# Alternating the units of two experts one by one inside a step of a two-expert SwiGLU loop

## The chip, the cores and the metric

The kernel runs on one core of a Trainium2 chip. The metric is the device time of one execution in microseconds, the median of several runs. The profile comes from one further execution.

## The reference, cut to what matters

The program is a two-layer decoder trunk on 256 tokens of width 1024. Layer 0 has windowed attention and a dense SwiGLU; layer 1 has dilated attention and a SwiGLU of eight experts, of which each token uses two. The change lies in the experts alone:

```python
def swiglu(h, w_gate, w_up, w_down):
    a = jnp.einsum('bsd,df->bsf', h, w_gate)
    b = jnp.einsum('bsd,df->bsf', h, w_up)
    return jnp.einsum('bsf,fd->bsd', jax.nn.silu(a) * b, w_down)

for e in range(N_EXPERTS):
    y = y + combine[..., e:e + 1].astype(h.dtype) * swiglu(h, w_gate[e], w_up[e], w_down[e])
```

All is float32. `D_FF` is 3584, so one expert has three matrices of 1024 x 3584.

## The kernel before, in words

**Three products for one.** A float32 product is made of fp32r products: each weight is split into a high part (`whi`, written by ScalarE in `cut`, line 548) and the rest (`wlo`, written by VectorE in its own `cut`, line 918, as raw minus `whi`). The activations have `xhi` and `xlo`, or `thi` and `tlo`. TensorE then forms hi x hi, hi x lo and lo x hi (`three`, lines 1470 to 1472).

**Units.** The weights are moved in units of 128 x 2048 values, 1 MB each. SyncE loads a unit into one of six `raw` buffers (line 414) as soon as VectorE has split the unit six places before (`lo_ready`). ScalarE splits it into one of four `whi` buffers, and waits for that until TensorE has finished the unit four places before (`units_done`); VectorE writes one of three `wlo` buffers, and waits for ScalarE's part (`hi_ready`) and for TensorE to have finished the unit three places before. TensorE waits for `lo_ready`.

**Pairs.** The experts are taken two by two, in four pairs here: a large one with up to 128 tokens and a small one with up to 64. A unit of the large expert is 12 matmuls of 512 columns (`unit_in`, `large_out`). For the small expert the high and the low part of the tokens stand side by side in one stationary tile, so its unit is 8 matmuls (`small_in` lines 1869 to 1873, `small_out` lines 1880 and 1881). A unit of either costs the same to load and to split.

**Steps.** 3584 columns are worked off in seven pieces of 512. Of each, an expert has two units of `moe_up`, two of `moe_gate` and two of `moe_down`. The loop `for s in 1..6` of every engine takes 12 units, called c to c+11 here with `c = MOE0 - 4 + 12 s`: up of piece s of the large expert (c, c+1), up of the small one (c+2, c+3), gate of the large (c+4, c+5), of the small (c+6, c+7), down of piece s-1 of the large (c+8, c+9) and of the small (c+10, c+11). A pair is eight units ahead of the loop, six steps, and four units behind it: 84 units.

**What hangs between the units.** The large expert: ScalarE `large_silu` (line 799) once its gate is done, VectorE `large_mul` (line 1365), TensorE `large_t` (four transposes, line 1919), ScalarE `large_thi` (line 804), VectorE `large_tlo` (line 1370). The small expert: `fold` at the end of a step (lines 1907 and 1911), VectorE `small_up` (line 1376), ScalarE `small_silu` (line 815), VectorE `small_mul` (line 1382), ScalarE `small_thi` (line 820), VectorE `small_tlo` (line 1388).

**What sets the order.** Every engine's order is written out by hand and is strict. In ScalarE's loop body the last three pieces are the split of c+12, `large_thi`, the split of c+13; in VectorE's the first are the split of c, `large_tlo`, the split of c+1, `small_up`, the split of c+2, `small_mul`, the splits of c+3 and c+4, `small_tlo`. So ScalarE's split of c+13 stands behind a wait for the transposes of `large_t`, and VectorE's split of the same unit (its c+1 of the next step) stands behind `large_tlo`.

```python
for i in range(11, 13):
    cut(c + i, rs)
large_thi(pair, s)
cut(c + 13, rs)
```

Of the kernel before, what the change touches and what calls it, by code (L numbers as in the profile page):

```python
# [35 lines left out]
STEPS = DFF // FCH  # L36
# [45 lines left out]
FIRST, FFN0, MOE0 = plan_units()  # L82
# [83 lines left out]
def trunk(nc, x, mem, rel_bias_table, mem_norm, norm_mix, norm_ffn, final_norm, swa_w_in, swa_sinks,  # L166
# [8 lines left out]
    moe_in = [w.rearrange("u p f -> p u f") for w in (moe_up, moe_gate)]  # L175
# [7 lines left out]
    with ctx:  # L183
# [221 lines left out]
        @block.sync  # L405
        def _(sp):
            for t in range(TILES):
                sp.dma_start(memx[:, t, :], mem[0, t * P:(t + 1) * P, :]).then_inc(mem_in[t], 16)

            def load(c, rounds, src):  # L410

                wait(sp, lo_ready, c + RAW * rounds - RAW + 1)
                dst = raw[:, c % RAW, 0:span(c)].rearrange("p (k f) -> p k f", k=src.shape[-2])
                sp.dma_start(dst, src).then_inc(raw_full[c % RAW], 16)

            def chunk_unit(k, i):

                name, width, rows_, off = CHUNKS[k]
                w = chunk_w[name]
                return bass.AP(w.tensor, w.offset + off * rows_ * P + i * P * 4 * width, [[4 * width, P], [1, 1], [1, 4 * width]])  # L420

            def load_chunks(lo, hi):
                for k in range(lo, hi):
                    for i in range(CHUNKS[k][2] // 4):
                        load(FIRST[k] + i, 0, chunk_unit(k, i))

            for half in range(2):
                piece = slice(half * 1024, half * 1024 + 1024)
                sp.dma_start(raw[:, 0:1, piece], chunk_unit(0, 0)[:, :, piece]).then_inc((first_in, raw_full[0])[half], 16)
            load(1, 0, chunk_unit(0, 1))  # L430
            load(2, 0, chunk_unit(1, 0))
            sp.dma_start(h[:, :, :], x[0].rearrange("(t p) d -> p t d", p=P)).then_inc(x_in, 16)
            sp.dma_start(gain[:, 1, :], bass.AP(gains[1].tensor, gains[1].offset, [[0, P], [1, D]]))\
                .then_inc(x_gain_in, 16)
            load(3, 0, chunk_unit(1, 1))
            load_chunks(C_SI, C_DI)

            for i in range(4):
                load(FFN0 + i, 0, ffn_in[i // 2][:, i % 2:i % 2 + 1, :])
            with sp.Fori(1, STEPS) as s:  # L440
                for i in range(4):
                    load(FFN0 - 2 + i, s, ffn_in[i // 2][:, bass.ds(2 * s + i % 2, 1), :])
                for i in range(2):
                    load(FFN0 + 2 + i, s, ffn_out[:, bass.ds(2 * s - 2 + i, 1), :])
            for i in range(2):
                u = 2 * STEPS - 2 + i
                load(FFN0 + FFN_UNITS - 2 + i, 0, ffn_out[:, u:u + 1, :])
            load_chunks(C_DI, len(CHUNKS))

            def load_in(c, rounds, first_unit):  # L450

                for i in range(4):
                    load(c + i, rounds, moe_in[i // 2][:, bass.ds(first_unit + i % 2, 1), :])

            def load_two(c, rounds, w, first_unit):

                for i in range(2):
                    load(c + i, rounds, w[:, bass.ds(first_unit + i, 1), :])

            def load_steps(pair, a, b):  # L460
                r = ROUNDS * pair
                load_in(MOE0 + 4, r, b)
                with sp.Fori(1, STEPS) as s:
                    for g in range(2):
                        load_two(MOE0 - 4 + 4 * g, r + 2 * s, moe_in[g], a + 2 * s)
                        load_two(MOE0 - 2 + 4 * g, r + 2 * s, moe_in[g], b + 2 * s)
                    load_two(MOE0 + 4, r + 2 * s, moe_out, a + 2 * s - 2)
                    load_two(MOE0 + 6, r + 2 * s, moe_out, b + 2 * s - 2)
                load_two(MOE0 + PAIR_UNITS - 4, r, moe_out, a + 2 * STEPS - 2)
                load_two(MOE0 + PAIR_UNITS - 2, r, moe_out, b + 2 * STEPS - 2)  # L470

            load_in(MOE0, 0, 0)
            sp.wait_ge(table_ready, 1)
            small = sp.value_load(jobs_i[0:1, 3:4], min_val=0, max_val=NE - 1)
            load_steps(0, 0, 2 * STEPS * small)
            sp.wait_ge(pairs_ready, 1)
            pairs = sp.value_load(jobs_i[0:1, 1:2], min_val=PAIRS, max_val=2 * PAIRS)
            with sp.Fori(1, pairs) as pair:
                large = sp.value_load(jobs_i[0:1, bass.ds(2 * pair + 2, 1)], min_val=0, max_val=NE - 1)
                small = sp.value_load(jobs_i[0:1, bass.ds(2 * pair + 3, 1)], min_val=0, max_val=NE - 1)  # L480
                load_in(MOE0, ROUNDS * pair, 2 * STEPS * large)
                load_steps(pair, 2 * STEPS * large, 2 * STEPS * small)
            for t in range(TILES):
                sp.wait_ge(hn_done, normed(5, t))
                sp.dma_start(out[0, t * P:(t + 1) * P, :], hn[:, t, :]).then_inc(out_done, 16)
            sp.wait_ge(out_done, 16 * TILES)
# [49 lines left out]
        def _(act):  # L536
# [259 lines left out]
            def large_silu(pair, s, unit):  # L796

                act.wait_ge(units_done, unit)
                act.activation(silu[:, 0, :], ps[:, B_GA, :], ACT.Silu).then_inc(silu_a, 1)
# [22 lines left out]
            def experts(pair, first=False, final=False):  # L822
# [22 lines left out]
                with act.Fori(1, STEPS) as s:  # L845
                    c, rs = MOE0 - 4, r + 2 * s
                    unit = pair_unit(pair, 12 * s - 4)
                    cut(c + 2, rs)
                    small_silu(pair, s - 1)
                    for i in range(3, 5):  # L850
                        cut(c + i, rs)
                    small_thi(pair, s - 1)
                    for i in range(5, 7):
                        cut(c + i, rs)
                    sums_of(0, unit + 3)
                    for i in range(7, 9):
                        cut(c + i, rs)
                    large_silu(pair, s, unit + 5)
                    for i in range(9, 11):
                        cut(c + i, rs)  # L860
                    sums_of(1, unit + 7)
                    for i in range(11, 13):
                        cut(c + i, rs)
                    large_thi(pair, s)
                    cut(c + 13, rs)
# [36 lines left out]
        def _(dve):  # L902
# [487 lines left out]
            def experts(pair, first=False, final=False):  # L1390
# [17 lines left out]
                with dve.Fori(1, STEPS) as s:  # L1408
                    c, rs = MOE0 - 4, r + 2 * s
                    cut(c, rs)  # L1410
                    large_tlo(pair, s - 1)
                    cut(c + 1, rs)
                    small_up(pair, s - 1)
                    cut(c + 2, rs)
                    small_mul(pair, s - 1)
                    for i in range(3, 5):
                        cut(c + i, rs)
                    small_tlo(pair, s - 1)
                    for i in range(5, 9):
                        cut(c + i, rs)  # L1420
                    large_mul(pair, s)
                    for i in range(9, 12):
                        cut(c + i, rs)
                if not final:
                    build_pick(pair + 1)
# [42 lines left out]
        def _(pe):  # L1468
# [453 lines left out]
            def large_out(c, rounds, half, final=False):  # L1922

                unit_out(c, rounds, [(thi[:, :, 0:P], tlo[:, :, 0:P])], half, final)

            def experts(pair, first=False, final=False):
# [19 lines left out]
                fold(pair, 0)  # L1946
                with pe.Fori(1, STEPS) as s:
                    c, rs = MOE0 - 4, r + 2 * s
                    for i in range(2):
                        unit_in(c + i, rs, 1, (B_UA,), i)  # L1950
                    pe.wait_ge(up_added, STEPS * pair + s)
                    for i in range(2):
                        small_in(c + 2 + i, rs, B_UB, i)
                    pe.wait_ge(tlo_a, STEPS * pair + s)
                    for i in range(2):
                        unit_in(c + 4 + i, rs, 1, (B_GA,), i)
                    pe.wait_ge(act_b, STEPS * pair + s)
                    for i in range(2):
                        small_in(c + 6 + i, rs, B_GB, i)
                    for i in range(2):  # L1960
                        large_out(c + 8 + i, rs, i)
                    large_t(pair, s)
                    pe.wait_ge(tlo_b, STEPS * pair + s)
                    for i in range(2):
                        small_out(c + 10 + i, rs, i)
                    fold(pair, s)
                pe.wait_ge(tlo_a, STEPS * pair + STEPS)
                for i in range(2):
# [49 lines left out]
```

## Time and profile before

| | |
|---|---|
| Median of 3 runs | 1370.68 us (1370.32 to 1371.89) |
| The profiled execution's own time | 1369.4 us |
| Its span | 1367.6 us |
| TensorE matmul busy | 1346.1 us (98%) |
| TensorE weight load busy | 1082.4 us (79%) |
| VectorE busy | 1130.5 us (83%) |
| ScalarE busy | 966.1 us (71%) |
| Mean granted TensorE clock | 0.998 |

The first 502 us are the first layer, the attention of the second and the routing; the rest of the span is the four pairs. Busy shares are of the whole span, so they mix the two. A matmul's recorded time overlaps the next one's; what a matmul costs is read from the starts of two that follow each other.

### The profile page before, as it was taken

The numbers are of one execution on the slowest core, as the hardware profiler recorded it, in microseconds if no ns is written. First come the engines' busy times: TensorE is split into PE (matmuls) and PEld (weight loads), VectorE is DVE, ScalarE is ACT, GpSimd is POOL, SyncE is SP. The second block draws the span as 40 slices with busy tenths as digits, with TensorE's granted clock in tenths as the row PEclk, the third lists the DMA queues.
The fourth block names the chain that finished last, engine by engine and source line by source line (L and its number), as shares of the span: only waits on it lengthen the run. The fifth ranks groups of instructions, "written<-read, shape, count | busy, mean of one in ns | idle before, by whom it ended". The sixth has DMA issues, their size and how long they took to land.

```text
span 1367.6 us, 19027 instructions
## 1 busy us (share of the span) xinstructions
PE 1346.1 (98%) x6561; PEld 1082.4 (79%) x6561; DVE 1130.5 (83%) x998; ACT 966.1 (71%) x904; POOL 13.7 (1%) x26
## 2 busy tenths in 40 slices
PE   9999999999999999999999999999999999999997
PEld 7888788888877887777777777788777778777775
DVE  6566555544554779999999999999999999999997
ACT  6553644433363468888887888887888887888886
POOL 1100000000000000000000000000000000000000
PEclk9999999999999999999999999999999999999999
DMA  9813655555451039999999999999999999999994
GB/s 374 307 56 113 222 191 187 184 184 186 152 215 62 18 145 414 423 422 422 422 421 366 410 422 422 421 422 369 395 422 421 421 422 398 378 422 423 422 422 173
DMA packets 61398, 433.21 MB, mean 317 GB/s; under 512 B 7066, under 2 KB 7241, under 8 KB 10032
## 3 DMA queue, kind: packets, MB, share of 16 engines
q1 hardware_dynamic: 59312, 426.80, 77.7%
q0 software_dynamic: 1888, 5.78, 1.3%
q8 instruction: 23, 0.38, 0.1%
q10 hardware_dynamic: 160, 0.14, 0.0%
q14 instruction: 15, 0.12, 0.0%
HBM read 431.60 MB, written 1.09 MB: 316 GB/s over the span
## 4 chain that ended last, share of the span: by engine, by line
PE 95%; DVE 3%; ACT 1%; issue 1%; ACTq 0%; DVEq 0%
PE ps L1470 20%; PE ps L1471 20%; PE ps L1472 20%; PE ps L1870 7%; PE ps L1869 7%; PE ps L1881 4%; PE ps L1880 4%; PE ps L1911 2%; PE ps L1599 1%; PE ps L1803 1%; PE ps L1572 1%; PE ps L1477 1%; PE ps L1872 1%; PE ps L1873 1%; PE ps L1919 1%; PE ps L1907 1%
## 5 line engine op out<-in xcount | busy, mean ns | idle before, releaser
L918 DVE TENSOR_TENSOR wlo<-raw,whi 128x2048 fp32r<-128x2048 f32 (+1 forms) x403 | 908.3, 2283 | 100.0 <-PE ps L1472 66.6
L548 ACT ACTIVATE whi<-raw 128x2048 fp32r<-128x2048 f32 (+1 forms) x403 | 764.7, 1915 | 111.2 <-PE ps L1472 53.9
L1470 PE MATMUL ps<-whi,xhi 128*128 128x512 f32 (+1 forms) x880 | 346.0, 393 | 4.7 <-DVE wlo L918 2.4
L1471 PE MATMUL ps<-wlo,xhi 128*128 128x512 f32 (+1 forms) x880 | 342.2, 389 | 0.0
L1472 PE MATMUL ps<-whi,xlo 128*128 128x512 f32 (+1 forms) x880 | 341.9, 388 | 0.0
L1470 PEld LDWEIGHTS ps<-whi,xhi 128*128 128x128 f32 x880 | 165.2, 188 | 42.3 <-DVE wlo L918 5.5
L1472 PEld LDWEIGHTS ps<-whi,xlo 128*128 128x128 f32 x880 | 165.2, 188 | 34.4
L1471 PEld LDWEIGHTS ps<-wlo,xhi 128*128 128x128 f32 x880 | 165.3, 188 | 32.4
L1870 PE MATMUL ps<-wlo,xhi 128*64 128x512 f32 x392 | 155.4, 396 | 0.0
L1869 PE MATMUL ps<-whi,xhi 128*128 128x512 f32 x392 | 153.3, 391 | 0.0
L1470 PE MATMUL ps<-whi,thi 128*128 128x512 f32 x320 | 125.9, 393 | 0.0
L1471 PE MATMUL ps<-wlo,thi 128*128 128x512 f32 x320 | 124.8, 390 | 0.0
L1472 PE MATMUL ps<-whi,tlo 128*128 128x512 f32 x320 | 124.8, 390 | 0.0
L1869 PEld LDWEIGHTS ps<-whi,xhi 128*128 128x128 f32 x392 | 73.6, 188 | 33.6
L1880 PE MATMUL ps<-wlo,thi 128*64 128x512 f32 x224 | 89.9, 401 | 1.4 <-DVE thi L1388 1.4
L1881 PE MATMUL ps<-whi,thi 128*128 128x512 f32 x224 | 87.9, 393 | 0.0
L1470 PEld LDWEIGHTS ps<-whi,thi 128*128 128x128 f32 x320 | 60.1, 188 | 13.1 <-DVE wlo L918 0.7
L1472 PEld LDWEIGHTS ps<-whi,tlo 128*128 128x128 f32 x320 | 60.1, 188 | 12.8
L1471 PEld LDWEIGHTS ps<-wlo,thi 128*128 128x128 f32 x320 | 60.1, 188 | 12.1
L1870 PEld LDWEIGHTS ps<-wlo,xhi 128*64 128x64 f32 x392 | 52.7, 134 | 17.6
L1881 PEld LDWEIGHTS ps<-whi,thi 128*128 128x128 f32 x224 | 42.1, 188 | 19.0
L643 ACT ACTIVATE silu<-ps,stats 128x512 f32<-128x512 f32 x14 | 9.7, 690 | 57.0 <-PE ps L1472 57.0
(249 smaller groups left out, 1094.7 us busy)
## 6 DMA issues: line engine op xcount, KB each, us to landing
raw<-in_moe_up SPq DMA_DIRECT2D x112, 1024.0 KB, 8.9
raw<-in_moe_gate SPq DMA_DIRECT2D x112, 1024.0 KB, 9.5
raw<-in_moe_down SPq DMA_DIRECT2D x112, 1024.0 KB, 9.2
raw<-in_ffn_up SPq DMA_DIRECT2D x14, 1024.0 KB, 4.8
raw<-in_ffn_gate SPq DMA_DIRECT2D x14, 1024.0 KB, 4.8
raw<-in_ffn_down SPq DMA_DIRECT2D x14, 1024.0 KB, 4.7
raw<-in_dil_w_in SPq DMA_DIRECT2D x10, 1024.0 KB, 4.8
raw<-in_swa_w_in SPq DMA_DIRECT2D x4, 1024.0 KB, 19.5
```

Source lines behind the costliest of these rows:

```text
L548: act.activation(whi[:, c % HIS, 0:span(c)], raw[:, c % RAW, 0:span(c)], ACT.Copy).then_inc(hi_ready, 1)
L918: dve.tensor_tensor(wlo[:, c % LOS, 0:n], raw[:, c % RAW, 0:n], whi[:, c % HIS, 0:n].bitcast(F32), ALU.subtract).then_inc(lo_ready, 1)
L1470: pe.matmul(dst, ahi, bhi, start=start, stop=False)
L1471: pe.matmul(dst, ahi, blo, start=False, stop=False)
L1472: return pe.matmul(dst, alo, bhi, start=False, stop=stop)
L1477: pe.matmul(ps[:, bank, 0:SEQ], ident, mats[:, 0:SEQ], start=True, stop=True)
L1572: last = pe.matmul(dst, qk[half, pair % 2, qb * P:(qb + 1) * P], qk[half, pair % 2, SEQ:SEQ + nk], start=True, stop=True)
L1869: pe.matmul(ps[:, bank, :], both, hi, start=kt == 0, stop=False)
L1870: last = pe.matmul(ps[0:HALF, bank, :], own, lo, start=False, stop=False)
L1880: pe.matmul(ps[0:HALF, B_Y[1][b], :], thi[:, ft, P:P + HALF], wlo[:, c % LOS, cols], start=False, stop=False)
L1881: return pe.matmul(ps[:, B_Y[1][b], :], thi[:, ft, P:2 * P], whi[:, c % HIS, cols], start=False, stop=stop)
L1911: last = pe.matmul(small_folded(1)[:, j * HALF:(j + 1) * HALF], small_sums(1)[:, j, :], both_halves[:, :], start=True, stop=True)
```

## The change

Inside the loop of steps the order of the units becomes large, small, large, small: c and c+2 are now the two up units of the large expert and c+1 and c+3 those of the small one; likewise c+4, c+6 and c+5, c+7 for the gate, c+8, c+10 and c+9, c+11 for the down matrix. SyncE loads them in that order (`load_turns`), and both splits follow, since they take units by number. The eight units ahead of the loop and the four behind it stay as they were. Three things move with the units: `large_silu` on ScalarE and `large_mul` on VectorE stand one split later, and `large_t` stands behind c+10 (it stood behind c+9). The waits `up_added`, `act_b` and `tlo_b` on TensorE stand one unit earlier.

```diff
+            def load_turns(c, rounds, w, large_unit, small_unit):
+                for i in range(2):
+                    load(c + 2 * i, rounds, w[:, bass.ds(large_unit + i, 1), :])
+                    load(c + 2 * i + 1, rounds, w[:, bass.ds(small_unit + i, 1), :])
...
# ScalarE
-                    for i in range(7, 9):
+                    for i in range(7, 10):
                         cut(c + i, rs)
-                    large_silu(pair, s, unit + 5)
-                    for i in range(9, 11):
-                        cut(c + i, rs)
+                    large_silu(pair, s, unit + 6)
+                    cut(c + 10, rs)
...
# VectorE
-                    for i in range(5, 9):
+                    for i in range(5, 10):
                         cut(c + i, rs)
                     large_mul(pair, s)
-                    for i in range(9, 12):
+                    for i in range(10, 12):
                         cut(c + i, rs)
...
# TensorE
-                    for i in range(2):
-                        unit_in(c + i, rs, 1, (B_UA,), i)
+                    unit_in(c, rs, 1, (B_UA,), 0)
                     pe.wait_ge(up_added, STEPS * pair + s)
-                    for i in range(2):
-                        small_in(c + 2 + i, rs, B_UB, i)
+                    small_in(c + 1, rs, B_UB, 0)
+                    unit_in(c + 2, rs, 1, (B_UA,), 1)
+                    small_in(c + 3, rs, B_UB, 1)
                     pe.wait_ge(tlo_a, STEPS * pair + s)
-                    for i in range(2):
-                        unit_in(c + 4 + i, rs, 1, (B_GA,), i)
+                    unit_in(c + 4, rs, 1, (B_GA,), 0)
                     pe.wait_ge(act_b, STEPS * pair + s)
-                    for i in range(2):
-                        small_in(c + 6 + i, rs, B_GB, i)
-                    for i in range(2):
-                        large_out(c + 8 + i, rs, i)
+                    small_in(c + 5, rs, B_GB, 0)
+                    unit_in(c + 6, rs, 1, (B_GA,), 1)
+                    small_in(c + 7, rs, B_GB, 1)
+                    large_out(c + 8, rs, 0)
+                    pe.wait_ge(tlo_b, STEPS * pair + s)
+                    small_out(c + 9, rs, 0)
+                    large_out(c + 10, rs, 1)
                     large_t(pair, s)
-                    pe.wait_ge(tlo_b, STEPS * pair + s)
-                    for i in range(2):
-                        small_out(c + 10 + i, rs, i)
+                    small_out(c + 11, rs, 1)
```

On TensorE, at the end of the loop body: before, the last matmul of c+9 is followed by `large_t` (it reads `act_h`) and by the first matmuls of c+10, a small unit with a second small unit behind it.

```order
L1472 MATMUL ps<-whi,tlo 128x512
L1917 REGISTER_ALU
L1919 MATMUL ps<-mats,act_h 128x128 [waits act_a]
L1919 MATMUL ps<-mats,act_h 128x128 x3
L1885 REGISTER_ALU [waits tlo_b]
L1880 MATMUL ps<-wlo,thi 64x512 [waits lo_ready]
L1881 MATMUL ps<-whi,thi 128x512
```

The same place of the changed kernel, where lines are numbered three higher:

```order
L1475 MATMUL ps<-whi,tlo 128x512
L1920 REGISTER_ALU
L1922 MATMUL ps<-mats,act_h 128x128 [waits act_a]
L1922 MATMUL ps<-mats,act_h 128x128 x3
L1888 REGISTER_ALU
L1883 MATMUL ps<-wlo,thi 64x512 [waits lo_ready]
L1884 MATMUL ps<-whi,thi 128x512
```

The last matmul shown ahead of the transposes is now that of c+10, and behind them stands one small unit, not two; the wait for `tlo_b` is gone from here and stands ahead of c+9.

On ScalarE, the end of the loop body is the same in both. This is the changed kernel (line 552 is the split, 808 is `large_thi`): the splits of c+11 and c+12, then the wait for `turned_a`, which `large_t` raises, then the split of c+13.

```order
L158 REGISTER_ALU [waits raw_full3]
L552 ACTIVATE whi<-raw 128x2048 [waits units_done]
L158 REGISTER_ALU [waits raw_full4]
L552 ACTIVATE whi<-raw 128x2048 [waits units_done]
L807 ISA
L808 ACTIVATE thi<-ps 128x4x128 [waits turned_a]
L158 REGISTER_ALU [waits raw_full5]
L552 ACTIVATE whi<-raw 128x2048 [waits units_done]
```

Nothing moved here, but the wait in the middle now ends behind another unit of TensorE.

On VectorE, from the split of c+8 on, before and then changed (917 and 921 are the split, 1368 is `large_mul`):

```order
L918 TENSOR_TENSOR wlo<-raw,whi 128x2048 [waits units_done,hi_ready]
L1364 ISA
L1365 TENSOR_TENSOR act_h<-ps,silu 128x512 [waits silu_a]
L914 REGISTER_ALU
L918 TENSOR_TENSOR wlo<-raw,whi 128x2048 [waits units_done,hi_ready]
```

```order
L921 TENSOR_TENSOR wlo<-raw,whi 128x2048 [waits units_done,hi_ready]
L917 REGISTER_ALU
L921 TENSOR_TENSOR wlo<-raw,whi 128x2048 [waits units_done,hi_ready]
L1367 ISA
L1368 TENSOR_TENSOR act_h<-ps,silu 128x512 [waits silu_a]
```

`large_mul` stands one split later; the number of splits ahead of c+10's is the same.

## Rows read from the trace of the kernel before

**Rows 1.** The page: busy time of TensorE, and bytes moved in 40 slices.
```profile
PE 1346.1 (98%) x6561; PEld 1082.4 (79%) x6561; DVE 1130.5 (83%) x998; ACT 966.1 (71%) x904; POOL 13.7 (1%) x26
GB/s 374 307 56 113 222 191 187 184 184 186 152 215 62 18 145 414 423 422 422 422 421 366 410 422 422 421 422 369 395 422 421 421 422 398 378 422 423 422 422 173
```

**Rows 2.** Busy time in two steps of the second pair; columns in the first line.
```profile
core 0: us, PE busy (x) PEld busy (x) DVE busy (x) ACT busy (x) POOL busy (x), PEclk, DMA share, GB/s
770.00:799.00 29.00, 29.00 (x137) 22.78 (x136) 28.74 (x18) 24.81 (x19) 0.00 (x0) 1.00 1.01 423
799.00:828.00 29.00, 29.00 (x136) 22.73 (x136) 28.74 (x17) 25.25 (x18) 0.00 (x0) 1.00 1.01 421
```

**Rows 3.** Waits from 525 to 1347 us: us in total, times, longest us.
```profile
ACT thi L804 <- PE ps L1919: 13.0, 16, 1.2
PEld ps L1470 <- DVE wlo L918: 2.4, 7, 0.5
```

**Rows 4.** The same view, 525 to 706 us, the first pair.
```profile
PEld ps L1470 <- DVE wlo L918: 0.9, 3, 0.5
```

**Rows 5.** TensorE's timeline, a step of pair two: start, us, line, operation.
```profile
798.77 0.48 PE L1470 MATMUL ps<-whi,xhi 128*128 128x512 f32 x1
...
801.60 0.39 PE L1470 MATMUL ps<-whi,xhi 128*128 128x512 f32 x1
...
804.32 0.39 PE L1869 MATMUL ps<-whi,xhi 128*128 128x512 f32 x1
...
808.02 0.39 PE L1470 MATMUL ps<-whi,xhi 128*128 128x512 f32 x1
...
822.65 0.60 PE L1919 MATMUL ps<-mats,act_h 128*128 128x128 f32 x4
823.00 0.48 PE L1880 MATMUL ps<-wlo,thi 128*64 128x512 f32 x1
...
828.01 0.48 PE L1470 MATMUL ps<-whi,xhi 128*128 128x512 f32 x1
```

**Rows 6.** ScalarE's timeline at the end of that step; idle time before in brackets.
```profile
823.28 0.60 ACT L804 ACTIVATE thi<-ps 128x512 fp32r<-128x512 f32 x1 [0.53 <-PE ps L1919]
823.77 3.95 ACT L548 ACTIVATE whi<-raw 128x2048 fp32r<-128x2048 f32 x2
```

**Rows 7.** VectorE's timeline over the same step.
```profile
796.72 2.28 DVE L918 TENSOR_TENSOR wlo<-raw,whi 128x2048 fp32r<-128x2048 f32 x1
...
799.52 2.28 DVE L918 TENSOR_TENSOR wlo<-raw,whi 128x2048 fp32r<-128x2048 f32 x1
...
802.05 2.28 DVE L918 TENSOR_TENSOR wlo<-raw,whi 128x2048 fp32r<-128x2048 f32 x1
804.59 2.29 DVE L918 TENSOR_TENSOR wlo<-raw,whi 128x2048 fp32r<-128x2048 f32 x1 [0.26 <-PE ps L1472]
806.80 0.42 DVE L1388 TENSOR_TENSOR thi<-small_h,thi 128x256 fp32r<-128x256 f32 x1
807.13 8.91 DVE L918 TENSOR_TENSOR wlo<-raw,whi 128x2048 fp32r<-128x2048 f32 x4
815.96 0.68 DVE L1365 TENSOR_TENSOR act_h<-ps,silu 128x512 f32<-128x512 f32 x1
816.56 8.89 DVE L918 TENSOR_TENSOR wlo<-raw,whi 128x2048 fp32r<-128x2048 f32 x4
```

**Rows 8.** Timelines of all three where TensorE waited, start of pair two.
```profile
712.33 3.72 ACT L548 ACTIVATE whi<-raw 128x2048 fp32r<-128x2048 f32 x2
714.36 4.50 DVE L918 TENSOR_TENSOR wlo<-raw,whi 128x2048 fp32r<-128x2048 f32 x2 [0.28 <-ACT whi L548]
716.71 0.50 PE L1470 MATMUL ps<-whi,xhi 128*128 128x512 f32 x1
...
719.57 0.39 PE L1470 MATMUL ps<-whi,xhi 128*128 128x512 f32 x1
```

**Rows 9.** Groups by line, 740 to 921 us: count, busy, mean ns, idle before.
```profile
L918 DVE TENSOR_TENSOR wlo<-raw,whi 128x2048 fp32r<-128x2048 f32 x74 | 166.7, 2285 | 2.8 <-ACT whi L548 1.6 <-PE ps L1472 1.2
L548 ACT ACTIVATE whi<-raw 128x2048 fp32r<-128x2048 f32 x74 | 141.1, 1918 | 17.2 <-PE ps L1472 5.6 <-DMA raw<-in_moe_down 4.6 <-DMA raw<-in_moe_up 2.8
```

**Rows 10.** The page: DMA issues, KB each, median us from issue to landing.
```profile
raw<-in_moe_up SPq DMA_DIRECT2D x112, 1024.0 KB, 8.9
```

More of the change, by code:

```diff
@@ L464, in load_steps @@
                     for g in range(2):
[L465 to L468, printed above, removed]
+                        load_turns(MOE0 - 4 + 4 * g, r + 2 * s, moe_in[g], a + 2 * s, b + 2 * s)
+                    load_turns(MOE0 + 4, r + 2 * s, moe_out, a + 2 * s - 2, b + 2 * s - 2)
                 load_two(MOE0 + PAIR_UNITS - 4, r, moe_out, a + 2 * STEPS - 2)
```

## The prediction

> **What bounds the kernel now.** I read the page first: matmuls are busy for 98% of the span, and from the seventeenth slice on the DMA moves 421 to 423 GB/s in most slices, and less only where pairs begin [rows 1]. Then the steps of the second pair by themselves: TensorE 29.00 us of 29.00 at full clock, VectorE 28.74, DMA saturated, ScalarE about 25 [rows 2]. Three resources are within 2% of one another, so I need to know which waits for which. TensorE hardly ever waits: 2.4 us in the whole expert part, seven times, always for the low split [rows 3], 0.9 us of it in the first pair [rows 4]. So TensorE's own work sets the pace there. Its step runs from 798.77 to 828.01, **29.24 us** [rows 5]: the first large unit 2.83, a large unit 2.72 (801.60 to 804.32), a small unit 1.85 (half of 804.32 to 808.02), `large_t` 0.35 (822.65 to 823.00). The DMA needs 12 x 1.0486 MB at 423 GB/s = 29.7 us for a step and VectorE's instructions, counted below, about 28.8. They keep up because a pair holds more than six steps: gather, scatter and transposes of the tokens cost TensorE time and the others little.
>
> VectorE waits only when TensorE has not yet freed a buffer (0.26 us before the split at 804.59 [rows 7]), and ScalarE waits for `large_t` 16 times, 13.0 us in all [rows 3]. That last wait is where the change strikes.
>
> **What stays.** The change adds no instruction on any engine, only new addresses, and twelve loads a step as before. TensorE's 120 large matmuls, transposes and folds are the same; in a step without a wait it is again 29.24 us long.
>
> **What comes earlier.** With small units in odd places, c+1, c+5 and c+9 end 2.72 - 1.85 = 0.87 us earlier, and their buffers come free by so much earlier; VectorE's 0.26 us before c+4's split goes. The price is that c+2 and c+6 are needed 0.87 us earlier, and c+10, ahead of which `large_t` no longer stands, 0.87 + 0.35 = 1.22 us earlier. Counted from the step's start, TensorE would like to begin c+1 at 2.83, c+2 at 4.68, c+4 at 9.25 (808.02 - 798.77), c+6 at 13.82, c+8 at 18.4 and c+10 at 23.0.
>
> **What comes later.** `large_t` began 5.36 us before the next step (822.65 against 828.01). It now has one small unit behind it and not two, so it begins 3.51 us before the next step: 1.85 us later. ScalarE already waited 0.53 us for it in this step [rows 6]. Behind that wait stands the split of c+13, and behind that VectorE's split of it, `small_up`, and all of the next step. I follow this chain from one `large_t` to the next:
>
> - ScalarE begins the split of c+13 1.12 us after `large_t` begins (822.65 to 823.77) [rows 5, 6].
> - The split takes 1.92 us [rows 9].
> - VectorE starts behind it. In the one place where my rows show VectorE following ScalarE, the split at 712.33 would end at 714.25 and VectorE starts at 714.36, 0.11 later [rows 8]. Nothing is the other bound; I take 0.05.
> - VectorE then goes from c+1 to the start of c+10 without a pause [rows 7]: split and `small_up` 2.80 (796.72 to 799.52), split and `small_mul` 2.53 (to 802.05), two splits at 2.21 each, `small_tlo` 0.33 (806.80 to 807.13), five splits at 2.21 = 11.04 (the four from 807.13 to 815.96 give 2.21 each), `large_mul` 0.60 (815.96 to 816.56). Sum 21.72.
> - TensorE's first matmul starts 2.35 us after the start of the split it waits for (714.36 to 716.71) [rows 8].
> - A large unit that begins behind a wait lasts 2.86 us (716.71 to 719.57) [rows 8], 0.14 more than one that doesn't, and then comes `large_t` again.
>
> Sum: 1.12 + 1.92 + 0.05 + 21.72 + 2.35 + 2.86 = **30.02 us**. Before, this chain had room, since `large_t` came 1.85 us earlier and c+10 was wanted 1.22 us later. Now it is longer than TensorE's 29.24, so it closes and sets the step. Laid beside TensorE's wishes: VectorE begins c+1 at -0.42, ends c+2 at 4.66 (wanted 4.68), c+4 at 9.39 (wanted 9.25: a wait of about 0.2), c+6 at 14.1 (wanted 14.2 by then), c+8 at 18.6 and c+10 at 23.6 (wanted 23.3). VectorE is idle about 1.1 us in each step before c+13, ScalarE more than before at `large_thi`.
>
> The rest lies beside this chain. `small_up` ends at 2.5 and is wanted at 2.83. `small_mul` and `small_tlo` end by 5 and 9.8; their waits stand now at c+5 (12.0) and c+9 (21). `large_mul` ends at 21.3, `large_t` wants it at 25.7. `large_silu` has its last unit 1.83 us later and stands one split, about 2.4 us, later. Each loses room and none is late; were VectorE's chain shorter, `small_up` would be late next.
>
> The loads: VectorE finishes c+1 about 1.6 us later than before, and with it the load of c+7 is issued later. A load lands 8.9 us after its issue [rows 10] and moves in 2.48, so more than two others stand ahead of it; the delay is taken from that queue. A step of 30.0 us is longer than the 29.7 us that the DMA needs, so it no longer falls behind within a pair.
>
> How often: the chain runs from one `large_t` of the loop to the next, five times in a pair's six steps; the first step starts from the transposes ahead of the loop, which have not moved, and behind the sixth the gather (32 matmuls of another kind) stands ahead of the small units. 4 pairs x 5 x (30.02 - 29.24 = 0.78) = **15.6 us**. Taken off: the waits of the first pair, 0.9 us [rows 4], where the DMA's arrears go; and 0.4 because the first interval of each of the four pairs still finds about 0.1 us of room (an estimate: VectorE's 0.26 us of idle time [rows 7], less than half of it). Net 14.3 us. The profiled execution took 1369.4 us (span 1367.6), so 1383.7 against it; the median of the runs is 1.3 us above that execution, so **1385.0 us**.
>
> Bounds for the unknown terms: without the 0.14 for a unit behind a wait and without the 0.05, the chain is 29.83 and the sum 20 x 0.59 - 0.9 = 10.9; if the chain also bites in four of five intervals only, 8.5. With 0.11 for 0.05 and the 0.14 paid at c+4 and c+6 as well, where these push c+10, it is 0.78 + 0.06 + 0.28 = 1.12 a step, 21.5 us. That is 1379 to 1392.
>
> **The rivals.**
>
> *The chain does not close.* ScalarE's split is 1.92 us and it idles 17.2 us in 740 to 921 [rows 9]; if in truth some of the 21.72 us overlap, or VectorE enters each pair so far ahead that five steps do not use it up, TensorE never waits. Against: VectorE is idle 2.8 us in those 181 us [rows 9], so its order has no room to catch up 1.85 us. Time: 1370.7 less at most the 2.4 us of rows 3: 1370. Chance 0.06.
>
> *Earlier release makes it faster.* VectorE, at 28.74 of 29.00 [rows 2], is taken as the engine that sets the pace; buffers freed 0.87 us earlier three times a step take away its idle time, 2.8 us in six steps [rows 9], 11 us in four pairs: 1360 us. It decides this way if matmuls could start closer than they do. Against: they follow one another with no idle time, and the waits that could go are 2.4 us [rows 3]. The Trainium skill (Perfetto Trace Analysis, Identifying the Most-Contended Engine) says that matmul busy share is no measure of TensorE's distance from its limit, that weight-load share is, and that occupancy names the engine to relieve; by it TensorE at 79% [rows 1] would not be the bound and VectorE would, and the time would be this rival's. Even a gain of a few us belongs here. Chance 0.03.
>
> *The DMA is starved too.* VectorE's pause before c+13 leaves 4.5 us between two releases of a raw buffer where the DMA needs 2.48. If the queue runs dry once a step, some 0.6 us are added: 20 x 0.6 = 12, 1397 us. For it: the DMA is saturated [rows 2]. Against: the 8.9 us from issue to landing [rows 10]. Chance 0.08.
>
> **The numbers.** Forecast 0.83 (it includes small closings of 3 us and more), starved 0.08, no closing 0.06, faster 0.03. A measurement of this kernel can tell about 0.2%, 2.7 us, from no change. The first two are slower, but for 0.01 of the forecast that may come out under 2.7 us; no closing is within. Faster 0.03, same 0.06 + 0.01 = 0.07, slower 0.83 + 0.08 - 0.01 = 0.90. The range, 1378 to 1393, takes in the bounds above with 1 us more on each side and leaves the rivals out.
>
> **What would show it.** In the profile after: in the second pair, steps of 30.0 us where they were 29.24; ScalarE's `thi` waiting for the transposes about 1 us or more in each of some 24 steps; VectorE's split waiting for ScalarE about 1 us once a step, 20 us or more in all against 1.6 in one pair now; weight loads of TensorE waiting for `wlo`, longest at the large units c+4 and c+10; the gaps between pairs unchanged. I am wrong if steps are 29.2 us long, if TensorE's waits stand at small units or behind `up_added`, or if ScalarE waits for the DMA rather than for TensorE.

## The result, and the profile after

| | before | changed |
|---|---|---|
| Median | 1370.82 us (4 runs, 1370.32 to 1371.89) | 1384.33 us (4 runs, 1384.20 to 1386.92) |
| Profiled execution, span | 1367.6 us | 1382.4 us |

The ratio is 1.0107, with a 95% interval of 1.0092 to 1.0121: the change makes the kernel slower by 13.5 us. Among the runs further down, one execution of `half_loads` took 1682.09 us at a mean granted clock of 0.847 and is left out of that kernel's median.

First, where the waits are. This is the view of waits of the changed kernel over its expert part (525 to 1361 us); its columns are those of [rows 3].

```profile
ACT thi L808 <- PE ps L1922: 79.6, 27, 3.4
PEld ps L1473 <- DVE wlo L921: 30.1, 85, 0.5
...
DVE wlo L921 <- ACT whi L552: 25.4, 28, 1.2
```

The last of these lines has this counterpart before (525 to 1347 us):

```profile
DVE wlo L918 <- ACT whi L548: 6.1, 26, 0.5
```

ScalarE's wait for the transposes of `large_t` grew from 13.0 us in 16 waits [rows 3] to 79.6 us in 27. VectorE waits for ScalarE about as often as before, 28 times and not 26, but now 25.4 us in all where it was 6.1: about one wait in each of the 24 steps, up to 1.2 us long and not 0.5. And TensorE's weight loads now wait 85 times for the low split, where there were seven such waits [rows 3].

Then one step, 801.95 to 831.97 us, which answers to [rows 5 to 7]. TensorE's timeline, from the `large_t` ahead of the step to the start of the next step:

```profile
798.42 0.60 PE L1922 MATMUL ps<-mats,act_h 128*128 128x128 f32 x4
...
801.95 0.48 PE L1473 MATMUL ps<-whi,xhi 128*128 128x512 f32 x1
...
806.72 0.50 PE L1473 MATMUL ps<-whi,xhi 128*128 128x512 f32 x1
...
811.46 0.50 PE L1473 MATMUL ps<-whi,xhi 128*128 128x512 f32 x1
...
816.20 0.50 PE L1473 MATMUL ps<-whi,xhi 128*128 128x512 f32 x1
...
825.60 0.51 PE L1473 MATMUL ps<-whi,thi 128*128 128x512 f32 x1
...
828.45 0.60 PE L1922 MATMUL ps<-mats,act_h 128*128 128x128 f32 x4
...
831.97 0.48 PE L1473 MATMUL ps<-whi,xhi 128*128 128x512 f32 x1
```

Four first matmuls have 0.50 or 0.51 us and not 0.39: those of c+2, c+4, c+6 and c+10. These are the places where TensorE waited for the low split; the first matmul behind a wait has this longer record also in [rows 8]. ScalarE and VectorE over the same stretch:

```profile
799.05 0.60 ACT L808 ACTIVATE thi<-ps 128x512 fp32r<-128x512 f32 x1 [3.26 <-PE ps L1922]
799.55 3.71 ACT L552 ACTIVATE whi<-raw 128x2048 fp32r<-128x2048 f32 x2
```

```profile
799.82 0.68 DVE L1373 TENSOR_TENSOR tlo<-ps,thi 128x512 fp32r<-128x512 f32 x1
801.57 2.29 DVE L921 TENSOR_TENSOR wlo<-raw,whi 128x2048 fp32r<-128x2048 f32 x1 [1.07 <-ACT whi L552]
803.78 0.68 DVE L1379 TENSOR_REDUCE small_h<-ps 128x256 f32<-128x512 f32 x1
804.38 2.28 DVE L921 TENSOR_TENSOR wlo<-raw,whi 128x2048 fp32r<-128x2048 f32 x1
...
806.92 4.48 DVE L921 TENSOR_TENSOR wlo<-raw,whi 128x2048 fp32r<-128x2048 f32 x2
811.32 0.42 DVE L1391 TENSOR_TENSOR thi<-small_h,thi 128x256 fp32r<-128x256 f32 x1
811.66 11.09 DVE L921 TENSOR_TENSOR wlo<-raw,whi 128x2048 fp32r<-128x2048 f32 x5
822.67 0.68 DVE L1368 TENSOR_TENSOR act_h<-ps,silu 128x512 f32<-128x512 f32 x1
823.27 6.68 DVE L921 TENSOR_TENSOR wlo<-raw,whi 128x2048 fp32r<-128x2048 f32 x3
```

ScalarE stands still for 3.26 us and then splits c+13 from 799.55 on. VectorE has its one pause of the step in front of the same unit, 1.07 us, and then none of over 0.15 us (the shortest that the view shows) until c+10's split at 823.27. The chain can be read term by term:

| from `large_t` to `large_t` | forecast | measured |
|---|---|---|
| `large_t` to ScalarE's split of c+13 | 1.12 | 799.55 - 798.42 = 1.13 |
| that split, and VectorE's start behind it | 1.92 + 0.05 | 801.57 - 799.55 = 2.02 |
| VectorE, c+1 to the start of c+10 | 21.72 | 823.27 - 801.57 = 21.70 |
| start of that split to TensorE's first matmul | 2.35 | 825.60 - 823.27 = 2.33 |
| c+10 on TensorE | 2.86 | 828.45 - 825.60 = 2.85 |
| sum | 30.02 | 828.45 - 798.42 = 30.03 |

The steps of all pairs, from one first matmul to the next, are as regular. Before, each took 29.24 to 29.27 us but the last of the first pair, 29.75. Changed, the first step of a pair took 29.28 us (29.48 in the first pair), and all the 20 that follow, 30.02 to 30.06.

How the 14.8 us between the two spans come together: 20 steps longer by 0.79 us on average, 15.7; less 0.5 for the step of 29.75, in which ScalarE had waited for a load ahead of 8 of its splits, 0.3 to 0.6 us each (that this lengthened the step I infer from `split_first_half` below); 0.2 for the first step of the first pair; 0.6 behind the last pair's last step; and 1.3 us less ahead of the experts, which is not the change's doing (below). These terms make 14.7.

The 0.6 us stand in TensorE's timeline at the very end, where the last small units of the last pair wait for `small_tlo`. Before:

```profile
1352.15 0.44 PE L1880 MATMUL ps<-wlo,thi 128*64 128x512 f32 x1 [1.39 <-DVE thi L1388]
```

and changed:

```profile
1366.94 0.44 PE L1883 MATMUL ps<-wlo,thi 128*64 128x512 f32 x1 [2.01 <-DVE thi L1391]
```

In the other pairs a gather stands between, and hides this.

### The profile page after: what moved, and what is told of

Its sections match the earlier page's. It is cut to its first block, busy times and chain, and to the rows that moved or that the text cites. A ratio compares the mean times of both kernels' runs of the same rounds, so it can differ in the third digit from the quotient of the medians.

```text
span 1382.4 us, 19027 instructions
## 1 busy us (share of the span) xinstructions
PE 1360.2 (98%) x6561; PEld 1075.3 (78%) x6561; DVE 1129.3 (82%) x998; ACT 952.9 (69%) x904; POOL 13.7 (1%) x26
## 4 chain that ended last, share of the span: by engine, by line
PE 95%; DVE 3%; ACT 1%; issue 1%; ACTq 0%; DVEq 0%
PE ps L1473 21%; PE ps L1474 20%; PE ps L1475 20%; PE ps L1873 7%; PE ps L1872 7%; PE ps L1883 4%; PE ps L1884 4%; PE ps L1914 2%; PE ps L1602 1%; PE ps L1806 1%; PE ps L1575 1%; PE ps L1480 1%; PE ps L1875 1%; PE ps L1876 1%; PE ps L1922 1%; PE ps L1910 1%
## 5 line engine op out<-in xcount | busy, mean ns | idle before, releaser
L1473 PE MATMUL ps<-whi,xhi 128*128 128x512 f32 (+1 forms) x880 | 352.9, 401 | 4.9 <-DVE wlo L921 2.4
L808 ACT ACTIVATE thi<-ps 128x512 fp32r<-128x512 f32 x28 | 16.7, 598 | 79.6 <-PE ps L1922 79.6
```

What stands on the lines that cost most here:

```text
L808: act.activation(thi[:, :, 0:P], ps[:, B_GA, :].rearrange("p (k t) -> p k t", k=FT), ACT.Copy)\
L1473: pe.matmul(dst, ahi, bhi, start=start, stop=False)
```

## The experiments

### Split first: the wait moved, the order kept

```diff
-                    large_thi(pair, s)
                     cut(c + 13, rs)
+                    large_thi(pair, s)
```

> The changed kernel, but ScalarE splits c+13 ahead of large_thi and not behind it. My theory: the chain from one large_t to the next loses ScalarE's wait and split (1.12 + 1.92 us), so it no longer closes; steps are back at 29.25 us (30.03 in the changed kernel) and the time at 1370 us, 1368.5 to 1372. Rival, the alternating order itself is what costs, since c+2, c+6 and c+10 are needed 0.9 to 1.2 us earlier: steps stay near 30 us and the time near 1384 us.

Measured: 1371.54 us median of 10 runs, ratio to before 1.0006 (0.9996 to 1.0015). Two lines on ScalarE give back the whole loss, with the alternating order in place. The waits of this kernel from 525 to 1340 us:

```profile
ACT thi L808 <- PE ps L1922: 9.6, 12, 1.2
PEld ps L1473 <- DVE wlo L921: 5.8, 19, 0.5
DVE wlo L921 <- ACT whi L552: 3.9, 12, 0.7
```

The 79.6, 30.1 and 25.4 us of the changed kernel are gone to 9.6, 5.8 and 3.9. In the three later pairs the steps are 29.26 to 29.30 us, but for the last of the fourth pair, 29.70. In the first pair the first step is 29.48, as in the changed kernel, and the last four are 29.47, 29.80, 29.80 and 29.79. These four are taken up below.

### Late turn: the wait moved, the order kept as before

```diff
-                    large_t(pair, s)
                     pe.wait_ge(tlo_b, STEPS * pair + s)
-                    for i in range(2):
-                        small_out(c + 10 + i, rs, i)
+                    small_out(c + 10, rs, 0)
+                    large_t(pair, s)
+                    small_out(c + 11, rs, 1)
```

> The kernel before, its units two by two, but large_t one small unit later (behind c+10). My theory: the same chain starts 1.85 us later and closes at c+4 or c+8, not at c+10: 1.12 + 1.92 + 0.05 + 7.54 on VectorE + 2.35, then units of 2.86, 2.74, 3.70, 5.46 and 1.85 us on TensorE make 29.6 us for a step, 20 x 0.35 = 7 us more than before: 1377 us, 1375 to 1379.5. Rival, the alternating order itself costs and the place of large_t nothing: 1370.8 us, steps of 29.25.

Measured: 1377.42 us, ratio 1.0057 (1.0041 to 1.0074). The steps two to six of each pair are 29.69 to 29.73 us, 0.1 more than the 29.6 worked out. Of the two candidates for the place of closing it is c+4: TensorE's first matmul follows VectorE's split directly (within 0.08 us) in 20 of 24 steps at c+4, and at no other unit of a step. (Weight loads wait for the low split for 0.13 to 0.22 us at c+3, c+8 and c+9 too; whether the 0.1 us more stands there I did not trace.) Its waits, 525 to 1340 us:

```profile
ACT thi L804 <- PE ps L1919: 60.0, 26, 3.1
...
DVE wlo L918 <- ACT whi L548: 18.1, 24, 1.2
PEld ps L1470 <- DVE wlo L918: 15.5, 44, 0.5
```

So `large_t` behind one more small unit costs 7 us with no alternation at all.

### Which units alternate

In one kernel only the up and gate units alternate, in the other only the down units.

```diff
# in_only: the changed kernel, with
-                    large_out(c + 8, rs, 0)
-                    pe.wait_ge(tlo_b, STEPS * pair + s)
-                    small_out(c + 9, rs, 0)
-                    large_out(c + 10, rs, 1)
-                    large_t(pair, s)
-                    small_out(c + 11, rs, 1)
+                    for i in range(2):
+                        large_out(c + 8 + i, rs, i)
+                    large_t(pair, s)
+                    pe.wait_ge(tlo_b, STEPS * pair + s)
+                    for i in range(2):
+                        small_out(c + 10 + i, rs, i)
```

and the down units loaded two by two. `out_only` is the kernel before with the opposite edit.

> Only the up and gate units alternate; the down units and large_t stand as before. My theory: large_t begins 5.36 us before the step's end as before, the chain stays open (27.7 us at its longest place), steps 29.25 us, time 1370 us, 1368.5 to 1371.5. Rival, the earlier need of c+2 and c+6 costs: two thirds of the loss, about 1379 us.

> Only the down units alternate, with large_t behind c+10; up and gate two by two. My theory: the whole loss is here, the chain through c+10 is the same 30.02 us: 1384 us, 1382 to 1386. Rival, the earlier need of three units costs: one third of the loss, about 1375 us.

Measured: `in_only` 1371.50 us (10 runs, ratio 1.0008, 0.9998 to 1.0017); `out_only` 1387.09 us (ratio 1.0123, 1.0106 to 1.0140). Alternating eight of the twelve units costs nothing that can be measured; alternating the other four costs all of it. Steps: 29.24 to 29.29 us in `in_only`, with one of 29.91; 30.03 to 30.09 for steps two to six in `out_only`. This is against the rival in which each of the three earlier needs costs its third, for two of them (c+2 and c+6) are in `in_only`. `out_only` came 1.1 us above the top of what I expected. Its profile shows why part of it is higher: the granted clock was at its lower level from 498.3 to 501.7 us, ahead of the experts, and the experts began at 503.6 us and not at 500.9.

### One operation more, on the chain and beside it

Each adds one operation to the changed kernel whose result nobody reads. The two copies on ScalarE have the same shape.

```diff
# thi_twice, behind the wait for turned_a
+                act.activation(hn[:, 0, 0:512], ps[:, B_GA, :], ACT.Copy)
# sums_twice, in sums_of for the gate
+                    act.activation(hn[:, 0, 512:1024], ps[:, B_GB, :], ACT.Copy)
# mul_twice, ahead of large_mul
+                dve.tensor_tensor(hn[:, 1, 0:512], ps[:, B_UA, :], silu[:, 0, :], ALU.mult)
```

> The changed kernel with one ScalarE copy of 128x512 from PSUM more (into memory that nobody reads), between the wait for large_t and large_thi. My theory: it lies on the chain, each of 20 intervals grows by its 0.5 to 0.6 us: 10 to 12 us more, 1395 us, 1393 to 1397. Rival, VectorE's own work or the DMA sets the step: no change, 1384 us.

> The same added ScalarE copy, but with sums_of for the small gate, between the splits of c+10 and c+11. My theory: ScalarE stands idle 2.9 us at large_thi in every step, so the copy only shortens that wait: 1384.3 us, 1383 to 1386. Rival, ScalarE's total work counts: 24 x 0.6 = 14 us more, 1398 us.

> The changed kernel with one VectorE product of 128x512 more, ahead of large_mul. My theory: it lies on the chain between c+1 and c+10, each of 20 intervals grows by 0.60 us: 12 us more, 1396 us, 1394 to 1398. Rival, VectorE is idle 1.1 us a step, so the time would not move: 1384 us.

| | median, us | ratio to before | steps 2 to 6 of a pair, us | ahead of the experts, us |
|---|---|---|---|---|
| changed kernel | 1384.33 | 1.0107 (1.0092 to 1.0121) | 30.02 to 30.06 | 500.9 |
| `thi_twice` | 1398.31 | 1.0201 (1.0184 to 1.0218) | 30.51 to 30.55 | 503.4 |
| `sums_twice` | 1386.97 | 1.0125 (1.0108 to 1.0142) | 30.02 to 30.07 | 503.1 |
| `mul_twice` | 1399.89 | 1.0218 (1.0201 to 1.0235) | 30.62 to 30.67 | 503.9 |

The step column decides: the copy adds 0.50 us to a step behind `large_t` and nothing between c+10 and c+11. Where it adds nothing, it only shortens the wait:

```profile
823.87 0.59 ACT L815 ACTIVATE hn<-ps 128x512 f32<-128x512 f32 x1
824.34 0.60 ACT L816 ACTIVATE silu<-ps 128x512 f32<-128x512 f32 x1
824.82 3.73 ACT L552 ACTIVATE whi<-raw 128x2048 fp32r<-128x2048 f32 x2
831.39 0.60 ACT L808 ACTIVATE thi<-ps 128x512 fp32r<-128x512 f32 x1 [2.84 <-PE ps L1924]
```

(ScalarE's timeline of `sums_twice`: 2.84 us of idle time where the changed kernel has 3.32 in the same step, at 829.08 us.) VectorE's product adds 0.61 us to a step though VectorE is idle 1.07 us in each, because the idle time lies ahead of the chain's part on VectorE and the product in it.

All three medians lie above what I expected, `thi_twice` by 1.3 us over the top of its interval, `sums_twice` by 1.0 and `mul_twice` by 1.9. The steps do not: 20 x 0.50 = 10 and 20 x 0.61 = 12.2 us. The rest is in the last column, 2.2 to 3.0 us ahead of the experts, and, for `thi_twice` and `mul_twice`, behind the last pair, 2.1 and 1.6 us. Both go with the granted clock, see below, but for 0.5 us at the end of `thi_twice`: the wait there is 2.50 us and not 2.01. `thi_twice` also has 0.9 us more between the pairs. In `mul_twice` the first step of the first pair grew too, from 29.48 to 30.66 us.

### Half loads: is it the DMA?

The loads of the loop's units move half the columns; the other half of every unit is stale.

```diff
-                    load(c + 2 * i, rounds, w[:, bass.ds(large_unit + i, 1), :])
+                    load_half(c + 2 * i, rounds, w[:, bass.ds(large_unit + i, 1), 0:UNIT // 2])
... (the small unit's load likewise)
```

> The changed kernel, but the loads of the loop's units move only the first half of each unit's columns; the splits and products then work on stale values in the other half. My theory: the DMA isn't on the chain: 1384 us, 1382.5 to 1385.5. Rival, the DMA queue runs dry at VectorE's pause and sets the step: back to 1370 to 1375 us.

> split_first with the loads of the loop's units halved (the other half of each unit is stale). In split_first the first pair's last four steps took 29.47 to 29.80 us and the last step of the fourth pair 29.70. My theory: these are the DMA's arrears (29.7 us for a step of loads), so with half the bytes all 24 steps take 29.25 to 29.3 us but for the first pair's first. Rival, they are a slower chain between the engines: they stay at 29.5 to 29.8 us.

`half_loads`, the changed kernel with half the bytes: 1386.75 us, ratio 1.0121 (1.0101 to 1.0141), steps of 30.02 to 30.05 us. Halving the traffic gives nothing back, and the steps are those of the changed kernel to 0.02 us; the median is 1.3 us above what I expected, and the profile shows 1.6 us more than that of the changed kernel at the end, where the clock fell (below). The DMA is not on the chain, and its queue running dry is out.

`split_first_half`, with the repair: 1367.82 us, ratio 0.9985 (0.9975 to 0.9994), and all steps 29.26 to 29.28 us but the first, 29.48. So the later steps of 29.47 to 29.80 us in `split_first` are the DMA's arrears; the first step's 29.48 is not. ScalarE's waits in the first pair show the same, first of `split_first`, then with half the bytes:

```profile
ACT whi L552 <- DMA raw<-in_moe_down: 7.9, 14, 0.9
ACT whi L552 <- DMA raw<-in_moe_up: 6.3, 13, 0.6
ACT whi L552 <- DMA raw<-in_moe_gate: 6.1, 13, 0.6
```

```profile
ACT whi L558 <- PE ps L1481: 8.9, 18, 0.6
ACT thi L814 <- PE ps L1928: 7.6, 6, 1.4
ACT silu L809 <- PE ps L1481: 4.9, 6, 0.9
```

### The repair without the alternation

The kernel before, with the two lines of `split_first` exchanged.

> The kernel before, with ScalarE's split of c+13 ahead of large_thi. The question is whether the repair is worth anything without the alternation. My theory: before, the chain has room and TensorE sets the step, so nothing moves but at most the 0.5 us by which the last step of the first pair is long: 1370 us, 1368.5 to 1371.5, steps 29.25. Rival, ScalarE's 13.0 us of waiting for large_t cost time before too: up to 13 us less, 1358 us.

Measured: 1371.69 us (12 runs), ratio 1.0009 (1.0000 to 1.0017): not faster, rather a touch slower. ScalarE's wait for `large_t` all but vanished (1.1 us in 3 waits from 525 to 1340 us, 13.0 before [rows 3]), and nothing came of it. Three pairs have steps of 29.24 to 29.27 us; in the first pair steps four to six took 29.67, 29.88 and 29.79. There the split of c+13 waits for its load, and now `large_thi` stands behind it; that this is the reason I did not test apart.

No version that loads all its bytes beat the kernel before. The best, `in_only` and `split_first`, stand within 0.1% of it, as they must: TensorE's steps are 29.25 us in all of them.

## Why the prediction was right

**The place.** I placed the cost at the split of c+13 behind the wait for `large_t`. `split_first` takes that away and the loss goes; `out_only` has it and has the loss; `in_only` does not have it and has none; `late_turn` has it without the alternation. Shown.

**The chain and its price.** 30.02 us forecast, 30.03 measured, with every term within 0.07 us (the table above). The largest miss is the 0.05 us between ScalarE's end and VectorE's start; it measured 0.12 (the split ended at 801.45), close to the bound that I had from [rows 8] (0.11). The two ends of VectorE's row were right to 0.02, since they came from the same instructions, with `large_mul` one split later among them.

**How often.** Five intervals a pair, 20 in all: yes, the first step of a pair is 29.28 us. I took off 0.4 us because the first interval would find some room; it found none (30.02 to 30.04 in all four), so this term should have been nothing. The 0.9 us for the waits of the first pair: 0.5 came, as the step of 29.75 went.

**What I had not counted.** The 0.6 us behind the last pair: I wrote that the gather stands ahead of the small units, and the last pair has no gather. The 0.2 us in the first step of the first pair. They weigh +0.8, the two terms above +0.8; the steps themselves gave 0.1 more than 15.6. Together the work of the change in the profiles is 16.0 us, where I had 14.3. Two things that have nothing to do with the change went the other way: the 1.3 us at the start, and the 1.3 us that I added because the median before lay so far above the profiled execution; changed, it lies 0.1 above (1384.33 against 1384.20). 1385.0 + 1.7 - 1.3 - 1.2 = 1384.2. That the total came within 0.7 us is therefore partly luck: the chain was right, and the terms beside it were off by 1.7 us.

**What TensorE does within a step.** I named c+4 and c+10. In the profile it waits at c+2, c+4, c+6 and c+10, 20 times or more at each, and its weight loads wait longest at c+2 (0.4 us), not at the two that I named. I had c+2 and c+6 at 0.02 to 0.1 us from the edge; behind a wait a unit is 0.13 us longer, and VectorE's 0.1 for 0.05 us tipped both. It costs nothing, because VectorE sets the chain.

**The rivals.** *No closing*: out, by the steps. *Earlier release makes it faster*: out, by `in_only`. There c+1 and c+5 are small units and hand back their buffers earlier, and the steps stay at 29.24 to 29.29 us. By the rule of the Trainium skill (Perfetto Trace Analysis, Identifying the Most-Contended Engine) VectorE would be the engine to relieve, and TensorE, at 79% weight loads, would have room. The runs speak against that here: with nearly all of TensorE's waits gone (`split_first_half`, 1.7 us in 5 waits for the low split) the step stays at 29.26 us, TensorE's own. *The DMA starves*: out, by `half_loads`. Its premise was too large as well: the two releases of a raw buffer around VectorE's pause are 803.86 - 799.90 = 3.96 us apart, not 4.5.

The late-turn run also checks the method on a second order: the same chain, traced to another unit, gave 29.6 us against 29.71 measured and 1377 us against 1377.4.

## What to carry to other kernels

When work is reordered on one engine, follow the events that it raises, not only its own inputs: here TensorE got its units more evenly, but an event moved 1.85 us later, and a split that had nothing to do with it stood behind that wait in another engine's strict order. Add up the ring from the event back to itself, with durations and starts from the trace; if the sum exceeds the present step, the difference times the number of rounds is the cost, and the idle time that shows up elsewhere is not to be had. Such a wait costs nothing while the ring is shorter than the step, and its whole excess in every round once it is longer; putting the unrelated operation ahead of the wait opens it again.

## What the runs showed of the hardware

**The clock moves the time of this kernel by 1 to 3 us, apart from any change.** The profiles show two places. First, the start. This is the stretch from 4 to 8 us of the kernel before and then of the changed one, in the columns of [rows 2]:

```profile
4.00:8.00 4.00, 4.00 (x19) 3.15 (x18) 0.00 (x0) 1.23 (x6) 0.00 (x0) 1.00 1.03 378
```

```profile
4.00:8.00 4.00, 4.00 (x27) 3.48 (x26) 0.85 (x4) 2.50 (x11) 0.00 (x0) 1.00 1.04 402
```

In the same 4 us, 19 matmuls began before and 27 in the changed kernel, the code being the same there; the profile's records have the clock at full from 7.3 us on in the one and from 4.1 us on in the other. (The column of the clock shows 1.00 in both, because it counts time without a record as full.) From then on TensorE's matmuls of the two profiles run about 1.25 us apart up to the experts. This is the 1.3 us above.

Second, between 496 and 504 us, where TensorE waits for the routing and transposes. `split_first` and the kernel before, in the same stretch:

```profile
496.00:504.00 8.00, 6.80 (x33) 6.80 (x34) 5.66 (x16) 2.76 (x5) 0.00 (x0) 0.57 0.51 190
```

```profile
496.00:504.00 8.00, 6.33 (x44) 5.63 (x43) 7.53 (x22) 5.42 (x9) 0.00 (x0) 1.00 0.41 152
```

The granted clock is 0.57 on average in one, the lower level (1.2 of 2.4 GHz) for 6.8 us of it, and 1.00 in the other. Five of the twelve profiles show such a fall, of 3.4 or 6.8 us, and in them the experts begin at 503.1 to 504.1 us; in the other seven at 500.9 to 502.2. The times of single runs fit: of the 23 of the kernel before that stand beside `before_split_first`, the four with a mean granted clock of 0.999 took 1367.64 to 1368.63 us, and the 19 with 0.996 to 0.998 took 1369.55 to 1372.59. The clock is not all of it: `before_split_first` itself took 1369.88 to 1374.78 us without such an order.

**A wait of 2 us near the end went with a fall of the clock in some profiles and not in others.** The changed kernel's 2.01 us wait ahead of the last small units left the clock at full in its own profile. In `half_loads`, at the same place, it fell:

```profile
1366.00:1370.00 4.00, 1.99 (x8) 1.32 (x8) 3.38 (x4) 2.54 (x4) 0.00 (x0) 0.89 0.00 0
1370.00:1374.00 4.00, 4.00 (x14) 2.79 (x13) 0.75 (x1) 1.07 (x2) 0.00 (x0) 0.68 0.00 0
```

The stretch from the last pair's last step to its last matmul took 13.20 us there, and 11.61 in the changed kernel. `thi_twice` and `mul_twice` show it too (13.68 and 13.18). Three of the seven profiles whose wait there is 2.0 us or longer show the fall, and none of the five in which it is 0.7 to 1.8 us. So when medians of such kernels differ by 1 to 3 us, the steps have to be read before a cause is named.
